# A four-layer block in one kernel: token factors applied behind the projections, context keys first, two thirds of the modulation on VectorE

## The reference, cut to what matters

```python
def rmsnorm(x, g):
    y = x * lax.rsqrt(jnp.mean(x * x, axis=-1, keepdims=True) + EPS)
    return y * g
def modulate(h, shift, scale):
    return h * (1 + scale) + shift
# layers 0 and 1: h = rmsnorm(x, g); h @ w_in  -> q, k, v, gate / latents, gate
# layer 2:
m = jax.nn.silu(cvec) @ w_mod + b_mod       # 6 groups of 1024; cvec is c, and c_ctx for the context
h  = modulate(rmsnorm(x, norm1_g), sh1, sc1);    q, k, v, hy_in, cf_in = split(h @ w_in)
hc = modulate(rmsnorm(ctx, norm1_g), csh1, csc1); kc, vc = split(hc @ w_in[:, 512:1536])
x = x + g1 * (concat([attn, hyena, conformer]) @ w_out)
x = x + g2 * experts(modulate(rmsnorm(x, norm2_g), sh2, sc2))
```

## Time and profile before

| | us |
|---|---|
| median of 3 runs | 1502.59 (1501.17 to 1505.56) |
| the profiled execution's own time | 1502.97 |
| its span | 1501.1 |
| TensorE busy | 1065.2 (71%) |
| VectorE busy | 446.9 (30%) |
| ScalarE busy | 292.7 (19%) |
| GpSimd busy | 110.2 (7%) |

### The profile page before, as it was taken

How to read it: one execution, slowest core, us unless ns; L and a number is a source line. 1 busy time by engine, 2 the same in 40 slices (tenths; PEclk the granted TensorE clock), 3 DMA queues, 4 the chain that set the end, 5 groups by cost and what they waited for, 6 DMA issues and landing times.

```text
span 1501.1 us, 15831 instructions
## 1 busy us (share of the span) xinstructions
PE 1065.2 (71%) x6826; PEld 570.6 (38%) x6826; DVE 446.9 (30%) x820; ACT 292.7 (19%) x492; POOL 110.2 (7%) x97
## 2 busy tenths in 40 slices
PE   6998999788998888666566565665565665655655
PEld 5886777465996775211111011111111110111112
DVE  5545656645595643011011011010110110110103
ACT  5335566344423431000000000000000000000001
POOL 1003400400522100000000000000000000000000
PEclk8999999898998988988888788788887888888788
DMA  9355067156517195999999999999999999999994
GB/s 313 128 198 195 18 244 278 33 228 225 190 42 204 16 390 227 430 428 429 427 430 428 429 429 427 429 429 428 428 429 427 428 430 428 429 428 428 430 428 189
DMA packets 70445, 486.76 MB, mean 324 GB/s; under 512 B 13831, under 2 KB 21544, under 8 KB 42472
## 3 DMA queue, kind: packets, MB, share of 16 engines
q1 hardware_dynamic: 69320, 484.71, 79.2%
q10 hardware_dynamic: 1056, 1.05, 0.2%
HBM read 484.69 MB, written 1.05 MB: 324 GB/s over the span
## 4 chain that ended last, share of the span: by engine, by line
DMA 57%; PE 30%; DVE 6%; ACT 3%; issue 2%; POOL 1%; SPq 0%; DVEq 0%; ACTq 0%
DMA ring<-in_expert_w 46%; PE ps L256 29%; DMA late<-in_expert_w 8%; DMA ring<-in_w_in 1%; DMA ring<-in_l_w_in 1%; DVE ring_r L311 1%; POOL hT L653 1%; DVE late L397 1%; DMA late<-in_rpb 1%; DVE hT L401 1%; ACT ring_r L303 1%; POOL hT L655 0%; ACT S L979 0%; DVE S L903 0%; SPq L1225 0%
## 5 line engine op out<-in xcount | busy, mean ns | idle before, releaser
L256 PE MATMUL ps<-ring,hT 128*32 128x512 f32 x688 | 115.1, 804 | 90.2 <-DMA ring<-in_expert_w 90.2
L256 PE MATMUL ps<-ring,G 128*32 128x512 f32 x672 | 113.9, 812 | 81.0 <-DMA ring<-in_expert_w 81.0
L256 PE MATMUL ps<-late_r,ring_r 128*128 128x256 f32 x832 | 154.5, 287 | 8.6 <-DVE hT_r L414 6.7
L256 PEld LDWEIGHTS ps<-late_r,ring_r 128*128 128x128 f32 x832 | 131.8, 192 | 12.0 <-issue 11.2
L256 PE MATMUL ps<-hT_r,ring_r 128*128 128x256 f32 x400 | 114.3, 286 | 0.0
L256 PE MATMUL ps<-U_r,ring_r 128*128 128x256 f32 x480 | 107.6, 285 | 0.1
L256 PE MATMUL ps<-late,U 128*128 128x256 f32 (+2 forms) x402 | 86.8, 505 | 22.4 <-DMA late<-in_expert_w 11.8
L311 DVE TENSOR_TENSOR ring_r<-ring,ring_r 128x2048 fp32r<-128x2048 f32 (+1 forms) x36 | 81.6, 2274 | 64.7 <-ACT ring_r L303 64.7
L256 PE MATMUL ps<-late,G 128*32 128x512 f32 (+1 forms) x384 | 66.6, 774 | 41.3 <-DMA late<-in_expert_w 41.2
L303 ACT ACTIVATE ring_r<-ring 128x2048 fp32r<-128x2048 f32 (+1 forms) x43 | 80.8, 1897 | 56.5 <-DMA ring<-in_l_w_in 30.7
L256 PEld LDWEIGHTS ps<-ring,hT 128*32 128x32 f32 x688 | 21.7, 130 | 181.8 <-DMA ring<-in_expert_w 142.5
(11 more groups left out here) (288 smaller groups left out, 1295.1 us busy)
## 6 DMA issues: line engine op xcount, KB each, us to landing
ring<-in_expert_w SPq DMA_DIRECT2D x128, 2048.0 KB, 40.9
late<-in_expert_w SPq DMA_DIRECT2D x64, 2048.0 KB, 40.9
ring<-in_w_mod SPq DMA_DIRECT2D x12, 2048.0 KB, 7.7
ring<-in_l_w_in SPq DMA_DIRECT2D x9, 2048.0 KB, 8.1
ring<-in_w_in SPq DMA_DIRECT2D x5, 2048.0 KB, 7.8
ring<-in_l_w_out SPq DMA_DIRECT2D x4, 2048.0 KB, 11.4
ring<-in_w_out SPq DMA_DIRECT2D x2, 2048.0 KB, 12.1
ring<-in_l_w_in SPq DMA_DIRECT2D x2, 1024.0 KB, 9.2
```

The source lines that it names most:

```text
L256: mm = lambda e, o, l, r, st, sp_=True, sk=False: e.matmul(o, l, r, start=st, stop=sp_, skip_group_check=sk)
```

## The change

- Layers 0 and 1: the tokens are split without the norm's factor, x times gain (`act_x_hi`, `dve_x_lo`), and projected at once. The factor is applied where a bank is emptied: q and k of layer 0 on VectorE with the factor as a row (`ev_qk`, moved there from ScalarE), v and the latents on ScalarE with the factor as a column per token (`r_col`, for which `pe_rms_all` has four narrow products more), the gates by a step of their own on VectorE (`dve_gate_r`) ahead of the tanh. The sum of squares stands behind the first group.
- The first pair of weights comes in two halves with semaphores of their own, each split and used as it lands; the constants' load goes behind the second and third pair.
- The context is loaded at the start into a tile of its own (CX). Its squares and factor are taken in layer 0, between groups 2 and 4; the rest once the modulation is there.
- Third layer: the order of the groups is now context k (30, 31), k (32, 33), context v (34, 35), v (36, 37), the third part of the Hyena input (38), conformer (39, 40), the rest of Hyena (41, 42), q (43, 44); the last norm's sum stands behind group 30. One pair serves k for context and tokens.
- Modulation: the first 2048 columns (four pieces) stay on TensorE. The other 4096 come transposed from the host, eight pieces of four times 1024 rows; VectorE multiplies each with silu(c), laid on all partitions, and sums it in one instruction (`dve_mod`, 32 in all). They are spread over layers 0, 1 and the start of the third.
- All splits leave GpSimd: high parts are ScalarE's, low parts VectorE's. Chunks 26 and 27 are split ahead of the latent attention loop, 28 and 29 in it; 41 to 44 in the grid attention loop.
- Bias loads for grid attention wait for group 35 instead of group 42.

```diff
+    pair(0, 1, 2, 3, 4)
+    mod(4)
+    pair(5, 6)
+    mod(5)
+    pair(7, 8)
+    mod(6)
     pair(9, 10)
-    mod(1, 2)
+    mod(7)
     pair(11, 12)
-    mod(3)
+    mod(8, 0)
     out.append(("Q", 0))
     pair(13)
+    mod(1)
     out.append(("K", 0))
-    mod(4, 5, 6, 7)
+    mod(2, 3, 9)
     pair(14, 15)
-    mod(8, 9, 10)
-    pair(16)
+    mod(10)
+    pair(16, 17)
     mod(11)
-    pair(*range(17, 24))
+    pair(*range(18, 24))
...
+    t(7, "gate_r", 0), t(8, "gate_r", 2)
...
+    t(16, "nqk", 0), t(16, "nqk", 2)
+    tok(17, "nv", 0, (2, 3, 0, 1))
+    t(18, "mix", 0), t(19, "mix", 2), t(20, "mix", 3)
+    t(21, "nqk", 4)
...
+    def act_x_hi(e, c, g, hi):
+        e.activation(r_(hi(c)), xc(c), ACT.Copy, scale=g(c)).then_inc(s["x_hi"], 1)
...
+    def dve_mod(e, m, i):
+
+        b = 4 * m + i
+        if i == 0:
+            wait_landed(e, ("M", m))
+        if m == 4 and i == 0:
+            e.wait_ge(s["row_d"], 1)
+        w = view(("M", m))[:, i, :]
+        e.tensor_tensor_reduce(w, w, SR[:, :], 0.5, p_("b_mod", b), ALU.mult, ALU.add,
+                               accum_out=mod[:, 2 * b:2 * b + 1]).then_inc(s["mod_d"], 1)
...
+    def dve_gate_r(e, nu, g, j):
+        e.tensor_tensor(v3(G, 8)[:, 2 * j:2 * j + 2, :], two(g % NB), row2(nu), ALU.mult).then_inc(s["gate_r"], 1)
+
+    def act_gate(e, n, j, tmp):
+        e.wait_ge(s["gate_r"], n + 1)
+        e.activation(tmp, G[:, 512 * j:512 * j + 512], ACT.Tanh, scale=0.5).then_inc(s["gate_t"], 1)
...
     def sp_program(e):
+        e.dma_start(PC[:, :], I["cols"]).then_inc(s["ld_pc"], 16)
+        src0 = piece_src(("W", 0))[0]
+        e.dma_start(w0h("W", 0), src0[:, 0:4, :]).then_inc(s["ld_w0"], 16)
+        e.dma_start(w0h("W", 1), src0[:, 4:8, :]).then_inc(slot_sem[0], 16)
+        issue(loads[2])
+        e.dma_start(SR[:, :], I["crow"].broadcast_to([128, 1024])).then_inc(s["ld_crow"], 16)
+        e.dma_start(CC[:, 128:], I["consts"][:, 128:]).then_inc(s["ld_cc"], 16)
+        e.dma_start(v3(CX, 8), I["ctxT"].rearrange("(c p) t -> p c t", p=128)).then_inc(s["ld_ctx"], 16)
...
     def pe_program(e):
-        pe_rms_sum(e, 0, ac)
+        pe_rms_sum(e, 0, vc)
+        pe_rms_all(e, 0)
+        pe_rms_sum(e, 1, gc)
+        pe_rms_all(e, 1)
...
-        pe_rms_sum(e, 1, sc)
-        pe_mod(e, 1)
-        pe_mod(e, 2)
+        pe_rms_sum(e, 2, sc)
+        pe_rms_all(e, 2)
...
-        pe_proj(e, 27, **XM)
-        pe_rms_sum(e, 2, vc)
-        pe_proj(e, 28, **XM)
-        pe_proj(e, 29, **XM)
+        for g in range(27, 30):
+            pe_proj(e, g, **XM)
+        pe_proj(e, 30, ready=x_ready(2), **XC)
-        for m in (8, 9, 10):
-            pe_mod(e, m)
-        pe_proj(e, 30, ready=x_ready(2), **X2)
-        pe_proj(e, 31, **X2)
-        pe_mod(e, 11)
-        for g in range(32, 39):
+        pe_rms_all(e, 3)
+        pe_proj(e, 31, **XC)
+        pe_proj(e, 32, ready=x_ready(3), **X2)
+        pe_proj(e, 33, **X2)
+        pe_tok(e, 34, **XC)
+        pe_tok(e, 35, **XC)
+        pe_tok(e, 36, **X2)
+        pe_tok(e, 37, **X2)
+        for g in range(38, 45):
-        pe_proj(e, 39, ready=x_ready(3), **XC)
-        pe_proj(e, 40, **XC)
-        pe_tok(e, 41, **XC)
-        pe_tok(e, 42, **XC)
-        pe_tok(e, 43, **X2)
-        pe_tok(e, 44, **X2)
+        pe_rms_all(e, 4)
+        pe_rms_all(e, 5)
...
     def act_program(e):
+        conv(3)
+        act_rms_root(e, 0)
+        conv(4)
+        act_crow(e)
+        e.wait_ge(s["row_d"], 1)
+        e.wait_ge(s["ld_ctx"], 16)
+            act_rms_sq(e, 1, c, cxc, gc)
+        conv(6)
+        conv(8)
+        act_rms_root(e, 1)
+        conv(12)
...
+            act_gate(e, j, j, gt0(j))
+        conv(18)
+        conv(20)
+            if g == 18:
+                conv(22)
+            for c in (2 * g - 32, 2 * g - 31):
+                e.wait_ge(s["res"], c + 1)
+                act_x_hi(e, c, lambda c: p_("l1_norm", c), ah)
+            for c in (2 * g - 32, 2 * g - 31):
+                act_rms_sq(e, 2, c, xc, sc)
+        act_rms_root(e, 2)
+        wait_col(e, 2)
+            e.activation(lat[t], bank[(20 + t) % NB][:, 0:448], ACT.Copy, scale=r_col(2, t, 1)).then_inc(s["lat"], 1)
...
+        act_mod(e)
+        conv(28)
+            if i == 5:
+                conv(29)
+            if i == 7:
+                conv(30)
...
+        act_mix(e, 0)
+        act_mix(e, 1)
+        conv(40)
+        act_mix(e, 2)
+        conv(41)
+        act_mix(e, 3)
+        act_mix(e, 4)
...
     def dve_program(e):
+        conv(2)
+        dve_rms_copy(e, 0)
+        conv(3)
+        dve_rms_inv(e, 0)
+        ev_qk(0)
+        conv(4)
+        dve_crow(e)
+        ev_qk(1)
+        conv(6)
+        dve_rms_copy(e, 1)
+        ev_qk(2)
+        conv(8)
+        dve_rms_inv(e, 1)
+        ev_qk(3)
+        dve_mod(e, 4, 0)
+        dve_mod(e, 4, 1)
+        ev_qk(4)
+        dve_mod(e, 4, 2)
+        dve_mod(e, 4, 3)
+        ev_qk(5)
+        conv(10)
+        ev_qk(6)
+        ev_qk(7)
+        dve_mod(e, 5, 0)
+        dve_mod(e, 5, 1)
+        conv(14)
+        dve_mod(e, 5, 2)
+        dve_mod(e, 5, 3)
+        conv(16)
+            dve_gate_r(e, 0, 12 + j, j)
+            dve_mod(e, 6, j)
+            if j:
+                dve_gate(e, j - 1, j - 1, gt0(j - 1))
+        dve_gate(e, 3, 3, gt0(3))
+        conv(18)
+        conv(20)
+            if g == 18:
+                conv(21)
+            if g == 19:
+                conv(22)
+            dve_mod(e, 7, g - 16)
+            for c in (2 * g - 32, 2 * g - 31):
+                dve_x_lo(e, 1, c, lambda c: p_("l1_norm", c), ah, hc)
+        dve_rms_copy(e, 2)
+        conv(23)
+        dve_rms_inv(e, 2)
...
+        dve_mod0(e)
+        dve_gain(e, 0, 1, 0, "norm1")
+        dve_gain(e, 1, 1, 1, "norm1")
+        for i in range(4):
+            dve_mod(e, 9, i)
+        conv(28)
+            if i in (5, 7):
+                conv(29 + (i > 5))
...
+        conv(36)
+        for i in range(4):
+            dve_mod(e, 11, i)
+        conv(37)
+        conv(39)
+        conv(41)
```

More of the change, by code:

```diff
@@ L347, in pe_tok @@
         W, H = view(("W", p)), view(("H", p))
-        for k in range(FIRST[p], FIRST[p + 1]):
-            e.wait_ge(s["w_lo_" + CHUNKS[k]["lo"]], CHUNKS[k]["lo_n"])
+        e.wait_ge(s["w_lo"], FIRST[p + 1] - 1)
         wait_group(e, g)
@@ L397, in dve_rms_inv @@
-        e.reciprocal(sm_r, sm_r).then_inc(s["rms_rc"], 1)
-        e.wait_ge(s["rms_rc"], nu + 1)
-    def dve_rms_out(e, nu, c, src, scale, out):
-        e.scalar_tensor_tensor(out(c), src(c), scale(c), sm_r, ALU.mult, ALU.mult).then_inc(s["rms_o"], 1)
-    def act_rms_split(e, nu, sg, hi, out, bias=None):
-        for c in range(8):
-            e.wait_ge(s["rms_o"], 8 * nu + c + 1)
-            if bias is None:
-                e.activation(r_(hi(c)), out(c), ACT.Copy).then_inc(s["x_hi"], 1)
-            else:
-                e.activation(r_(hi(c)), out(c), ACT.Identity, bias=bias(c)).then_inc(s["x_hi"], 1)
@@ L411, in dve_low @@
-    def dve_low(e, sg, c, hi, out, bias=None):
-        e.wait_ge(s["x_hi"], 8 * sg + c + 1)
-        if bias is None:
-            e.tensor_tensor(r_(out(c)), out(c), r_(hi(c)), ALU.subtract).then_inc(s["x_lo"], 1)
-        else:
-            e.scalar_tensor_tensor(r_(out(c)), out(c), bias(c), r_(hi(c)), ALU.add, ALU.subtract).then_inc(s["x_lo"], 1)
-    def dve_rms_all(e, nu, sg, src, scale, hi, out, bias=None):
-        for c in range(8):
-            dve_rms_out(e, nu, c, src, scale, out)
-            if c:
-                dve_low(e, sg, c - 1, hi, out, bias)
-        dve_low(e, sg, 7, hi, out, bias)
+        e.wait_ge(s["rms_rt"], ROOTS[nu])
@@ L425, in x_ready, with dve_h_lo @@
+    def dve_h_lo(e, sg, c, hi, out, bias):
+        e.wait_ge(s["x_hi"], 8 * sg + c + 1)
+        e.scalar_tensor_tensor(r_(out(c)), out(c), bias(c), r_(hi(c)), ALU.add, ALU.subtract).then_inc(s["x_lo"], 1)
     def x_ready(sg):
@@ L476, in act_mod, with pe_mod_tr, dve_mod0 @@
-    def act_mod(e, g):
-        e.wait_ge(s["mod_p"], 4 * g + 4)
-        if g:
-            e.wait_ge(s["mod_t"], g)
+    def pe_mod_tr(e):
+        e.wait_ge(s["mod_a"], 1)
+        for j in range(4):
+            k = e.transpose(bank[5][:, j * 128:(j + 1) * 128], mtmp[:, j * 128:(j + 1) * 128], c_("ident"))
+        k.then_inc(s["mod_t"], 1)
+    def act_mod(e):
+        e.wait_ge(s["mod_p"], 4)
         e.activation(mtmp, bank[5][:, :], ACT.Copy).then_inc(s["mod_a"], 1)
-    def dve_mod(e, g):
+    def dve_mod0(e):
@@ L497, in dve_gain @@
     def dve_gain(e, j, group, col, name):
-        e.wait_ge(s["mod_d"], 2 * (group // 2) + 2)
+        if group < 2:
+            e.wait_ge(s["mod_0"], 2)
+        else:
+            e.wait_ge(s["mod_d"], 8 * (group - 1))
         e.scalar_tensor_tensor(gs[:, 8 * j:8 * j + 8], modv[:, group, :, col], 1.0, p_(name, 0, 8),
@@ L2102, in pool_program @@
         e.memset(CF[:, :, 271:286], 0.0).then_inc(s["pad"], 1)
-        for k in range(35, 41):
```

(1 more changed line is left out.)

451 lines of the change are left out of this document (224 added, 227 removed).

## The result

The changed kernel takes 1527.33 us (median of 4 runs, 1526.89 to 1527.79) where the kernel before takes 1502.07 in the runs beside it: a ratio of 1.0164, 95% interval 1.0146 to 1.0181, so 25 us slower. Measured once more in the last series it gives 1526.31 us and 1.0159 [1.0144, 1.0175]. The forecast was 1522 with a range of 1497 to 1532.

A forecast was written before the change was run, and what follows sets the result against it. The expert tail only slides; the front, with TensorE the bound in long stretches and elsewhere waiting on a three-engine chain, sets the change. Its shifts run to +19.7 us at w_out_2's first product: 1522 us, range 1497 to 1532.

The forecast's parts named there:

- The start is given back: Kernel start: first product at 10.4 us, but waits on ScalarE leave group 3 ending at 44.5, as before at 44.0.
- VectorE's queue in layer 0: Before filter step 5, TensorE waits 9.6 us for VectorE's steps behind two new low parts; groups 6 and 7 end +12.7.
- Into stick-breaking: Two high parts behind ScalarE's filter evacuations and their low parts delay VectorE's first step there: 151.0 for 133.07, +17.9 us.
- Layer 1: Group 20 waits 2.5 us for a low part, group 22 stalls 6.7 behind the root; group 23's end +20.5.
- Into latent attention: Four modulation steps and two low parts ahead of VectorE's first maximum, 8.4 us beyond the old lead: +28.0.
- The loop: Latent attention loop: two splits add 5.9 us, missing transposes give back 3.1; group 26 at 346.9 for 316.08.
- Groups 26 to 29: They run without the two norm stages between them, 4 × 5.75 us, done at 370.0; the delay falls to +23.4.
- Context first: Third layer: short filter and taps start only behind group 42, TensorE idles; grid attention's first maximum 480.2 for 461.54, +18.7.
- The grid loop: Grid attention loop: two low parts come forward, +1.0 us; w_out_2's first product at 549.9 for 530.21.
- VectorE's queue is no bound: Rival on the front: VectorE reaches the filter step before 64 us and stalls fall away, 1497 us; chance 0.16.
- It cancels: Rival on the front: half the stalls, or the modulation's 15 us of TensorE all on the path, 1502 to 1507; chance 0.10.
- The sum at half rate: Rival on VectorE's modulation: each multiply-and-sum costs 2.29 us, +1.1 each, +13 on the path, 1535 us; chance 0.08.

The follow-up runs named there:

- Run 1: Changed kernel with VectorE's steps of filter stages 4 and 5 put ahead of two low parts: 1520.5 us, ratio 1.0111.
- run 2: Changed kernel with ScalarE's two high parts for the output projection moved ahead of the last gate, one low part earlier on VectorE: 1522.58 us, ratio 1.0126.
- Run 3: Changed kernel with ScalarE's two high parts for groups 22 and 23 ahead of the norm's root: 1518.4 us, ratio 1.0102.
- run 7: Kernel before, with the split of chunks 26 and 27 moved from GpSimd to ScalarE and VectorE, into latent attention: 1497.92 us, ratio 0.9975.
- run 6: Changed kernel with the 32 multiply-and-sums of the modulation cut from 1024 elements to 8: 1522.77 us, ratio 1.0145.
- Run 5: Changed kernel with the third layer's groups that feed short filter and taps earlier, taps ahead of short filter, loads and bias loads reordered: 1512.83 us, ratio 1.0080.
- Run 11: Changed kernel with the weight splits around the grid attention placed as in the kernel before: 1523.93 us, ratio 1.0137.
- runs 1 to 4: Single reorders of the changed kernel; the fourth moves sums and low parts ahead of latent attention's first maximum into VectorE's waits: 1518.27 us, ratio 1.0096.
- run 8: Kernel before, keeping one product of eight in each of the eight modulation pieces the change takes from TensorE: 1504.31 us, ratio 1.0011.
- run 10: Changed kernel with five reorders plus four more, among them the context's squares ahead of the first norm's root: 1487.36 us, ratio 0.9905.
- runs 5, 9 and 10: Changed kernel with reordered taps; the middle one has all five reorders of the first five runs together: 1490.39 us, ratio 0.9914.

## Why the prediction was right, and where its terms were off

**The start is given back: right.** First product at 11.66 (10.4 forecast), group 3's end at 45.04 (44.5). I had left out ScalarE's table load of 1.28 us ahead of its first high part.

**VectorE's queue in layer 0: right, mechanism and place.** Idle time before filter step 5 7.62 (9.6 forecast), released by the step on S. Filter step 8 +13.7 (13.1). Run 1 shows that it is the order.

**Into stick-breaking: right.** +18.8 for VectorE's first step (17.9); run 2 takes 5.0 us of TensorE's wait there away by order alone.

**Layer 1: right.** Idle times of 2.51 and 6.66 (2.5 and 6.7); group 23's end +20.7 (20.5); first up-projection evacuation at 258.21 (258.1). Run 3.

**Into latent attention: the sum was too large by 4.** First maximum +23.9 (28.0 forecast). GpSimd's release gave what I said: k's two scalings and the step ahead of them took 2.96 for 10.65 us, 7.7 less (7.6 forecast), and run 7 shows it alone. Two terms were too large. "A mod piece and four gate steps add 3.5" measured +1.4, from the first evacuation to the step ahead of the scalings (34.0 us for 32.6); run 6, without the sums, leaves this stretch at 34.0, so the sums are no part of it. And behind the scalings, where I had 8.4, it was 6.3; 1.6 of this is that the transposes of k took 2.1 us at a granted clock of 1.00, where in the kernel before they took 3.7 at 0.50.

**The loop: too small.** 36.9 us for 32.5, +4.4, where I had +2.8 (5.9 less 3.1). Run 7 has the two splits alone and gives +5.0, so the 5.9 was about right; the term that failed is "the missing transposes give back 3.1", which gave 0.6. It came from rows of TensorE, which is not what ends a step of this loop.

**Groups 26 to 29: right in kind.** VectorE's residual of group 29 starts at 368.81, 0.70 behind the product, so they end at 368.1 (370.0 forecast), 23.7 us for four (23.0).

**Context first: right in place, 3.3 too small from group 29's end on.** First maximum of the grid attention at 481.60 (480.2), TensorE idle for 20.84 (19.8), but the stretch began 1.9 us earlier than forecast. Run 5 shows that the order of groups, loads and steps is the cause. Two things I had not seen. ScalarE waits here for a load, 7.92 us for w_in_2 columns until 438.13, and VectorE behind it for 8.60; from then on VectorE has no idle time (0.4 us in all) until the first maximum at 481.60. How much of the 20.84 us this wait makes, no run isolates. And the bias additions on GpSimd now fall beside the short filter, three of whose steps take 1.4 to 1.6 us for 0.48, together 3.0 us on that unbroken path, for which the forecast had nothing; in the kernel before VectorE had nothing to do beside them (timeline of VectorE in the changed kernel):

```profile
440.56 0.43 DVE L1124 SCALAR_TENSOR_TENSOR late<-late 128x256 f32<-128x256 f32 x1 [8.60 <-ACT late L1116]
...
448.83 1.40 DVE L1134 SCALAR_TENSOR_TENSOR late<-G,PC,late 128x256 f32<-128x256 f32 x1
...
451.62 1.57 DVE L1134 SCALAR_TENSOR_TENSOR late<-G,PC,late 128x256 f32<-128x256 f32 x1
...
455.44 1.43 DVE L1134 SCALAR_TENSOR_TENSOR late<-G,PC,late 128x256 f32<-128x256 f32 x1
```

**The grid loop: too small.** +3.1 (+5.4 in the second profile) where the forecast had +1.0 for the two low parts brought forward. Run 11 puts this stretch back to 68.7 us with the splits in their old places.

Together: +23.1 at group 45 for a forecast of +19.7. That the sum is off by only 3.4 is partly luck: 4.3 too much into latent attention stand against 1.6 too little in its loop, 3.3 in front of the grid attention and 2.1 in its loop. **The rivals:** "VectorE's queue is no bound" falls by all of runs 1 to 4. "It cancels" needed half of the stalls gone, or TensorE's 15 us on the path; the stalls came as large as forecast, and run 8 finds nothing of the 15. "The sum at half rate" would have been 2.29 us or more an instruction; it is 1.28, and even the removal of all 32 gains 3 us. The Trainium skill (Vector Engine (DVE) Microarchitecture Reference, Points that are easy to get wrong) was weighed there as the rule that halves throughput; this case's trace does not show that for 1024 elements.

## What to carry to other kernels

When work moves to an engine whose queue has a fixed order, ask of each new instruction when its inputs are there and who stands behind it; the sum of its busy time says little. Here 40 us of new work cost 3 us, and 4.6 us of low parts, waiting for a high part, cost 5. When a group order is changed to hide one chain, look for the long chain that lost its cover. A part is priced between its own start and end: in run 7 a gain ahead of the loop hides the 5 us that the splits cost in it. And before an operation is moved forward, look up when its load lands, as run 10 did not.

## What the runs showed of the hardware

GpSimd and VectorE hold each other up by whole instructions here, in both directions. In the kernel before, VectorE's scaling of k took 5.51 us; its GpSimd neighbour ran from 268.92 to 273.74, and 5.51 from 269.31 ends at 274.82, which is the neighbour's end and 1.1 us, close to the 1.22 of run 7. The step ahead, 2.38 us for 0.69, ends at 269.38, 0.5 behind the end of its own GpSimd neighbour. In the changed kernel GpSimd's addition of a bias, 1.29 us beside single steps of the short filter (1.26 in the kernel before, with VectorE idle), took 20.09 beside the unbroken taps (timeline of GpSimd):

```profile
455.30 1.29 POOL L1311 TENSOR_TENSOR late<-late 128x512 f32<-128x512 f32 x1 [2.39 <-DMA late<-in_rpb]
462.72 20.09 POOL L1311 TENSOR_TENSOR late<-late 128x512 f32<-128x512 f32 x1 [6.12 <-DMA late<-in_rpb]
```

It ends at 482.81, 1.1 us behind the last step of the taps (481.07 and 0.61). By the Trainium skill (SBUF — State Buffer, "SBUF: two separate sides"), the port pair that the two engines share is held for a whole instruction and the other one waits; the traces agree. Whether GpSimd gets in between back-to-back steps of VectorE varies. In both profiles of the changed kernel and in runs 1 to 4, 6 and 11 one addition took 18.3 to 22.6 us beside some 50 taps. In runs 5, 9 and 10, with the taps as close behind each other, the first addition took 3.7 to 4.0 us, and the others beside taps 1.3 to 1.6, for each of which one tap took 1.5 us in place of 0.47 (run 5, timeline of GpSimd):

```profile
449.44 1.52 POOL L1314 TENSOR_TENSOR late<-late 128x512 f32<-128x512 f32 x1 [1.90 <-DMA late<-in_rpb]
```

What decides between the two, no run shows.
